# Summing the gathered value rows four units at a time, with seven row buffers and four weight buffers

## The chip, the core and the metric

The kernel runs on one core of a Trainium2 chip, as one launch. Its time is the device time of that core in microseconds (us). Five engines work in parallel and meet at semaphores: TensorE (PE in the profile; PEld is its weight load), VectorE (DVE), ScalarE (ACT), GpSimd (POOL) and SyncE (SP), which only issues loads. TensorE's granted clock can be 1.2 or 2.4 GHz; in this profile it is at the full 2.4 GHz through all of the stage that the change touches.

## What is computed

One step of a decoder layer, for 256 prompt tokens and for 8 x 4 sample tokens that read a paged cache of 2048 rows:

```python
h = rmsnorm(x); q, k, v, qi, ki, wi, cx, cb, cc, ga, gb = split(h @ w_in)
idx = top_k(relu(qi . ki) weighted by wi)            # 256 rows for each sample token
p   = softmax(q . k[idx] + bias)                     # 8 heads
out = sum over the 256 rows of p * v[idx]            # the step that is changed
x   = x + (sigmoid(ga) * (out @ w_pa) + sigmoid(gb) * (conv @ w_pb)) @ w_o
x   = x + square(relu(rmsnorm(x) @ w1)) @ w2
```

All of it is float32. The prompt's attention is dense with a mask, and is computed head by head.

## The kernel before

**The product with w_in.** h @ w_in is made in 44 pairs of column tiles (`pairs`, `win_half`, L397 and on), 256 columns each. A pair is eight chunks of the weights (128 x 512, two of the 16 rows of tiles). float32 is split into a high and a low part: ScalarE copies a chunk into its high part VH (`highs`, L849), and VectorE or GpSimd subtracts it to get the low part VL (`lows`, L1428 on VectorE, L1712 on GpSimd). TensorE then runs twelve matmuls of 288 columns on the chunk (L406 high x high, L407 high x low, L408 low x high). VH and VL have four buffers, so the high part of chunk u waits until chunk u - 4 is used. In pairs 30 to 37 VectorE makes the low parts of the odd chunks and GpSimd those of the even ones (`dve_low`). The SyncE queue loads the chunks of the next pair as the low parts of this one are done.

**The selected rows.** A sample token's 256 rows lie spread over the 128 partitions (4 partitions a token, 32 tokens) in 64 *units*: one unit is one row of 1024 floats in each partition, fetched by an indirect DMA of GpSimd (`gather`, L1715 and on, issued at L1726), 0.5 MB. First come 64 units of keys (up to pair 29), then 64 units of values. `kv` is a ring of five such row buffers (RK = 5). `knrep` and `vnrep` are two more tiles of that size, which hold the new keys and values of the sample tokens.

**Summing the values.** For unit v VectorE writes a *spread* (`spread_unit`, L1498): a tile `sp` of 128 x 256, in which the softmax weight of each partition stands in the column of its token and head. TensorE multiplies it with the rows (`unit_sum`, L780 to L785): eight heads, each a matmul with 32 columns of weights and 128 of data, accumulated in one bank; a head appears as two instructions in the trace (16 per unit, L783). `sp` is a ring of two. A unit zero, the new values in `vnrep`, comes ahead of unit 0.

**The order.** Everything is in the engines' program order. TensorE calls `after(j)` behind chunk j of each half of a pair, and `values_at` (L793) sums the units v - 1 and v behind every odd j: a group of two units behind every second chunk, 32 groups in pairs 30 to 37. After the second half of a pair (and at half of it) there are short attention matmuls of the prompt (L744, L745: logits; L391: transposes; L759, L760: output). VectorE goes through the same chunks c of a pair: behind every even c it writes two spreads, then the low parts up to chunk c + 3, then other work: in pair 30 the rest of a top-k over the mask (`prompt_top`), in pairs 31 and on at c = 1 and c = 5 the prompt's softmax (`prompt_row`, `prompt_scale`), in pairs 31 and 32 at c = 2, 3, 6 and 7 the convolution (`conv_tile`, L1533 to L1537) and at the end of 32 a product with the gate (L1565). The spread for unit v waits until unit v - 2 is summed. GpSimd makes the low parts up to chunk v + 4 of the stage and then issues the gather for unit v + 5 once unit v is summed. The semaphore `unit_summed` counts the sums, the one of `vnrep` included.

Of the kernel before, what the change touches and what calls it, by code (L numbers as in the profile page):

```python
# [13 lines left out]
P = 128  # L14
# [31 lines left out]
RK = 5  # L46
# [69 lines left out]
def build(nc, I, O):  # L116
    with ExitStack() as ctx:
# [54 lines left out]
        sp = sb("sp", [P, 2, H, NS])  # L172
# [86 lines left out]
        def const(name, rows=P):  # L259
# [19 lines left out]
            "unit_read conv_done tmax_ready tmax_turned tmax_wide tmax_back lg_shifted lg_exp lsum_ready lsum_wide "  # L279
# [5 lines left out]
        ks = [ctx.enter_context(nc.semaphore(f"rows_in{i}")) for i in range(RK)]  # L285
# [8 lines left out]
        C_MLP = C_WO + 16  # L294

# [89 lines left out]
        def _(pe):  # L385
# [377 lines left out]
            def tops(j):  # L763
                if j == 3:
                    pe.wait_ge(S["ul_copied"], 2)
                    pe.wait_ge(S["tmax_ready"], 1)
                    transpose(bank(4, 0, P, H), small[:, 0:H]).then_inc(S["tmax_turned"], 1)

            def sums(j):
                if j == 0:  # L770
                    pe.wait_ge(S["tmax_wide"], 1)
                    transpose(bank(7, 0, H), smx).then_inc(S["tmax_back"], 1)
                elif j == 3:
                    pe.wait_ge(S["lsum_ready"], 1)
                    pe.matmul(bank(5, 0, H), const("b4"), small[:, 16:16 + H], start=True, stop=True).then_inc(S["lsum_wide"], 1)
# [11 lines left out]
            def v_unit(v):  # L787
                n = UNITS + v
                pe.wait_ge(S["sp_ready"], v + 2)
                pe.wait_ge(ks[n % RK], 16 * (n // RK + 1))  # L790
                unit_sum((1 + v) % 2, kv[:, n % RK, :])

            def values_at(p, half):  # L793
                def after(j):
# [4 lines left out]
                    if j % 2 and v < UNITS:  # L799
                        v_unit(v - 1)  # L800
                        v_unit(v)
# [416 lines left out]
        def _(dve):  # L1218
# [264 lines left out]
            dve.tensor_reduce(small[:, 0:H], byh, AX_X, ALU.max).then_inc(S["tmax_ready"], 1)  # L1483
            lows(UNIT * (VP - 1) + 4)
            dve.wait_ge(S["tmax_turned"], 1)
            step(dve.tensor_reduce(smt, bank(4, 0, P, H).rearrange("p (n s) -> p n s", s=4), AX_X, ALU.max))
            dve.tensor_copy(smx.rearrange("p (n s) -> p n s", s=4), smt.unsqueeze(2).to_broadcast([H, NS, 4])).then_inc(S["tmax_wide"], 1)
            dve.wait_ge(S["tmax_back"], 1)
# [3 lines left out]
            dve.tensor_reduce(small[:, 16:16 + H], byh, AX_X, ALU.add).then_inc(S["lsum_ready"], 1)  # L1492
            dve.wait_ge(S["lsum_wide"], 1)
# [6 lines left out]
            def spread_unit(v):  # L1500

                if v:
                    dve.wait_ge(S["unit_summed"], v)
                spread((1 + v) % 2, lg[:, v, :].unsqueeze(2).to_broadcast([P, H, NS]))
# [359 lines left out]
```

## Time and profile before

| | |
|---|---|
| median of 3 runs | 1791.46 us (1788.7 to 1793.67) |
| profiled execution | 1791.65 us, span 1789.9 us |
| mean granted clock of TensorE | 0.990 |
| TensorE busy | 98% of the span |
| VectorE, ScalarE, GpSimd busy | 58%, 39%, 32% |
| moved by DMA | 348.53 MB, 195 GB/s over the span |
| value stage (first sum to the end of the last) | 509.3 to 664.0 us |

A row of the timeline gives the start in us from the start of the span, the duration, the engine, the line of the kernel, what is written and read, the shapes, and in brackets the idle time of the engine ahead of it with what ended it. Matmuls are pipelined: one starts while the one before it still runs, and the end of each is modelled, so the distance of the starts tells the pace, not the durations. "busy" of TensorE therefore also covers short breaks of its rhythm.

### The profile page before, as it was taken

The numbers are of one execution on the slowest core, as the hardware profiler recorded it, in microseconds if no ns is written. First come the engines' busy times: TensorE is split into PE (matmuls) and PEld (weight loads), VectorE is DVE, ScalarE is ACT, GpSimd is POOL, SyncE is SP. The second block draws the span as 40 slices with busy tenths as digits, with TensorE's granted clock in tenths as the row PEclk, the third lists the DMA queues.
The fourth block names the chain that finished last, engine by engine and source line by source line (L and its number), as shares of the span: only waits on it lengthen the run. The fifth ranks groups of instructions, "written<-read, shape, count | busy, mean of one in ns | idle before, by whom it ended". The sixth has DMA issues, their size and how long they took to land.

```text
span 1789.9 us, 32474 instructions
## 1 busy us (share of the span) xinstructions
PE 1751.0 (98%) x13712; PEld 1701.0 (95%) x13712; DVE 1039.0 (58%) x1147; ACT 690.1 (39%) x845; POOL 563.9 (32%) x450
## 2 busy tenths in 40 slices
PE   9999999999999999999999999999999999999997
PEld 8859998999888999999999999999999999999996
DVE  4559997889989432255456554455444554455543
ACT  5534443543344555433333332233323332233332
POOL 3718778888866667400231000000000000000001
PEclk9999999999999999999999999999999999999998
DMA  6725457988879974654454444444444444444442
GB/s 211 239 66 156 153 166 256 349 296 295 306 263 316 337 275 152 209 182 159 167 187 156 165 164 165 164 165 163 166 163 165 164 164 165 164 165 164 163 165 100
DMA packets 73793, 348.53 MB, mean 195 GB/s; under 512 B 8978, under 2 KB 11154, under 8 KB 52660
## 3 DMA queue, kind: packets, MB, share of 16 engines
q1 hardware_dynamic: 50112, 268.00, 44.0%
q0 software_dynamic: 19584, 71.31, 11.4%
q10 hardware_dynamic: 3988, 7.66, 1.2%
q8 instruction: 81, 1.33, 0.3%
q14 instruction: 28, 0.23, 0.0%
HBM read 340.50 MB, written 6.44 MB: 194 GB/s over the span
## 4 chain that ended last, share of the span: by engine, by line
PE 86%; DVE 10%; POOL 2%; DMA 1%; issue 1%; ACT 0%; POOLq 0%; DVEq 0%; ACTq 0%
PE PM L426 19%; PE PM L428 19%; PE PM L427 19%; PE PM L406 8%; PE PM L408 7%; PE PM L407 7%; PE PM L391 2%; DVE lg L1438 2%; DVE kv L1433 2%; DVE VL L1428 2%; PE PM L783 1%; DMA kv<-cache_v,offs 1%; POOL VL L1712 1%; POOL kv L1726 1%; DVE sp L1498 1%
## 5 line engine op out<-in xcount | busy, mean ns | idle before, releaser
L849 ACT ACTIVATE WH<-wring 128x2048 fp32r<-128x2048 f32 (+1 forms) x163 | 307.3, 1885 | 679.9 <-PE PM L428 676.1
L1582 DVE TENSOR_TENSOR WL<-wring,WH 128x2048 fp32r<-128x2048 f32 x159 | 364.5, 2292 | 341.3 <-ACT WH L849 341.2
L406 PE MATMUL PM<-hH,VH 128*128 128x288 f32 x1408 | 428.9, 305 | 11.1 <-POOL VL L1712 6.9
L1712 POOL TENSOR_TENSOR VL<-wring,VH 128x512 fp32r<-128x512 f32 x292 | 383.4, 1320 | 163.5 <-ACT VH L849 147.8
L407 PE MATMUL PM<-hL,VH 128*128 128x288 f32 x1408 | 418.7, 297 | 0.0
L408 PE MATMUL PM<-hH,VL 128*128 128x288 f32 x1408 | 417.3, 296 | 0.0
L426 PE MATMUL PM<-XH,WH 128*128 128x288 f32 x1280 | 379.1, 296 | 1.5 <-DVE WL L1589 1.5
L426 PE MATMUL PM<-YH,WH 128*128 128x288 f32 x1280 | 379.4, 296 | 0.0
L427 PE MATMUL PM<-YL,WH 128*128 128x288 f32 x1280 | 377.6, 295 | 0.0
L427 PE MATMUL PM<-XL,WH 128*128 128x288 f32 x1280 | 377.6, 295 | 0.0
L428 PE MATMUL PM<-XH,WL 128*128 128x288 f32 x1280 | 376.3, 294 | 0.0
L428 PE MATMUL PM<-YH,WL 128*128 128x288 f32 x1280 | 376.3, 294 | 0.0
L849 ACT ACTIVATE VH<-wring 128x512 fp32r<-128x512 f32 x352 | 221.7, 631 | 336.7 <-PE PM L408 336.2
L406 PEld LDWEIGHTS PM<-hH,VH 128*128 128x128 f32 x1408 | 267.2, 190 | 24.6 <-POOL VL L1712 8.9
L408 PEld LDWEIGHTS PM<-hH,VL 128*128 128x128 f32 x1408 | 268.2, 190 | 0.0
L407 PEld LDWEIGHTS PM<-hL,VH 128*128 128x128 f32 x1408 | 267.6, 190 | 0.2
L1767 POOL TENSOR_SCALAR ysam<-ysam,small 32x1024 f32<-32x1024 f32 x2 | 6.2, 3122 | 824.1 <-DVE small L1688 824.1
L426 PEld LDWEIGHTS PM<-XH,WH 128*128 128x128 f32 x1280 | 239.8, 187 | 1.8 <-ACT G L926 1.7
L428 PEld LDWEIGHTS PM<-XH,WL 128*128 128x128 f32 x1280 | 241.0, 188 | 0.0
L428 PEld LDWEIGHTS PM<-YH,WL 128*128 128x128 f32 x1280 | 241.0, 188 | 0.0
L427 PEld LDWEIGHTS PM<-XL,WH 128*128 128x128 f32 x1280 | 240.2, 188 | 0.1
L427 PEld LDWEIGHTS PM<-YL,WH 128*128 128x128 f32 x1280 | 240.2, 188 | 0.0
(267 smaller groups left out, 1574.4 us busy)
## 6 DMA issues: line engine op xcount, KB each, us to landing
wring<-w_in SPq DMA_DIRECT2D x176, 512.0 KB, 4.6
wring<-w_mlp_in SPq DMA_DIRECT2D x64, 1024.0 KB, 5.2
wring<-w_mlp_out SPq DMA_DIRECT2D x64, 1024.0 KB, 5.2
wring<-w_o SPq DMA_DIRECT2D x16, 1024.0 KB, 5.2
wring<-w_pb SPq DMA_DIRECT2D x8, 1024.0 KB, 4.9
wring<-w_pa SPq DMA_DIRECT2D x8, 1024.0 KB
xT<-x_t SPq DMA_DIRECT2D x1, 2304.0 KB, 12.2
bias_scratch<-uv ACTq DMA_DIRECT2D x8, 192.0 KB, 4.6
```

Source lines behind the costliest of these rows:

```text
L391: return pe.transpose(out, in_, cp[0:n, 0:n])
L406: pe.matmul(out, vh, hH[:, k, :], start=(k == 0), stop=False)
L407: pe.matmul(out, vh, hL[:, k, :], start=False, stop=False)
L408: m = pe.matmul(out, vl, hH[:, k, :], start=False, stop=(k == KT - 1))
L426: pe.matmul(out, wh, rh[:, k0 + k, :], start=(first and k == 0), stop=False)
L427: pe.matmul(out, wh, rl_[:, k0 + k, :], start=False, stop=False)
L428: m = pe.matmul(out, wl, rh[:, k0 + k, :], start=False, stop=(last and k == CK - 1))
L849: return act.activation(out, in_, ACT.Copy, **kw)
L1428: dve.tensor_tensor(VL[:, u % 4], r, VH[:, u % 4], ALU.subtract).then_inc(S["vl_dve"], 1)
L1433: m = dve.tensor_tensor(by2, by2, PM[:, 6:8, :], ALU.mult)
L1582: dve.tensor_tensor(WL[:, i % 2], wring[:, i % 2], WH[:, i % 2], ALU.subtract).then_inc(S["wl_ready"], 1)
L1712: pool.tensor_tensor(VL[:, u % 4], r, VH[:, u % 4], ALU.subtract).then_inc(S["vl_pool"], 1)
```

## The change

`sp` gets four buffers instead of two. TensorE sums four units behind chunk j = 3 of each half (16 groups) instead of two behind each odd chunk. VectorE writes four spreads at c = 0 and c = 4, each as soon as the unit four before it is summed. The value rows get seven buffers: the five of `kv`, then `knrep` and `vnrep` (`v_row`). GpSimd now issues the gather for unit v behind the low parts up to chunk v - 3 of the stage, once unit v - 7 is summed; units 5 and 6 are the first to go to `knrep` and `vnrep`. Seven semaphores of the softmax are replaced by two that count. No arithmetic is changed or moved to another engine.

```diff
@@ -169,7 +169,7 @@
-        sp = sb("sp", [P, 2, H, NS])
+        sp = sb("sp", [P, 4, H, NS])
@@ -276,13 +276,13 @@
-            "unit_read conv_done tmax_ready tmax_turned tmax_wide tmax_back lg_shifted lg_exp lsum_ready lsum_wide "
+            "unit_read conv_done soft_ready soft_turned lg_shifted lg_exp "
-        ks = [ctx.enter_context(nc.semaphore(f"rows_in{i}")) for i in range(RK)]
+        ks = [ctx.enter_context(nc.semaphore(f"rows_in{i}")) for i in range(RK + 2)]
@@ -292,6 +292,14 @@
+
+        def v_row(v):
+
+            r = v % (RK + 2)
+            if r < RK:
+                at = (UNITS + r) % RK
+                return kv[:, at, :], ks[at], 16 * (-(-(UNITS - at) // RK) + v // (RK + 2) + 1)
+            return (knrep if r == RK else vnrep)[:], ks[r], 16 * (v // (RK + 2) + 1)
@@ -763,16 +771,16 @@
-                    pe.wait_ge(S["tmax_ready"], 1)
-                    transpose(bank(4, 0, P, H), small[:, 0:H]).then_inc(S["tmax_turned"], 1)
+                    pe.wait_ge(S["soft_ready"], 1)
+                    transpose(bank(4, 0, P, H), small[:, 0:H]).then_inc(S["soft_turned"], 1)
...
@@ -785,10 +793,10 @@
                 m.then_inc(S["unit_summed"], 1)
             def v_unit(v):
-                n = UNITS + v
+                rows, arrived, count = v_row(v)
                 pe.wait_ge(S["sp_ready"], v + 2)
-                pe.wait_ge(ks[n % RK], 16 * (n // RK + 1))
-                unit_sum((1 + v) % 2, kv[:, n % RK, :])
+                pe.wait_ge(arrived, count)
+                unit_sum((1 + v) % 4, rows)
             def values_at(p, half):
                 def after(j):
@@ -796,9 +804,9 @@
                     if v == 0:
                         pe.wait_ge(S["sp_ready"], 1)
                         unit_sum(0, vnrep[:], True)
-                    if j % 2 and v < UNITS:
-                        v_unit(v - 1)
-                        v_unit(v)
+                    if j == 3 and v < UNITS:
+                        for i in range(4):
+                            v_unit(v - 3 + i)
                 return after
             for p in range(VP, AP0 + H + 1):
...
@@ -1499,9 +1507,9 @@
             def spread_unit(v):
-                if v:
-                    dve.wait_ge(S["unit_summed"], v)
-                spread((1 + v) % 2, lg[:, v, :].unsqueeze(2).to_broadcast([P, H, NS]))
+                if v >= 3:
+                    dve.wait_ge(S["unit_summed"], v - 2)
+                spread((1 + v) % 4, lg[:, v, :].unsqueeze(2).to_broadcast([P, H, NS]))
             def prompt_row(h):
@@ -1542,9 +1550,9 @@
             for p in range(VP, AP0 + H):
                 for c in range(UNIT):
                     v = UNIT * (p - VP) + c
-                    if c % 2 == 0 and v < UNITS:
-                        spread_unit(v)
-                        spread_unit(v + 1)
+                    if c % 4 == 0 and v < UNITS:
+                        for i in range(4):
+                            spread_unit(v + i)
                     lows(UNIT * p + c + 4)
                     if p == VP:
                         if c < TOPP // 8 - 2:
@@ -1714,17 +1722,24 @@
             def gather(n):
-                src, u = ("cache_k", n) if n < UNITS else ("cache_v", n - UNITS)
-                if RK <= n < UNITS + RK:
-                    k, added = n - RK, sum(m <= n - RK for m in ACT_UNITS)
+                if n >= RK:
+                    k = n - RK
+                    added = sum(m <= k for m in ACT_UNITS)
                     if k in ACT_UNITS:
                         pool.wait_ge(S["unit_added"], added)
                     else:
                         pool.wait_ge(S["unit_read"], k + 1 - added + (k > NEWKEY))
-                elif n >= UNITS + RK:
-                    pool.wait_ge(S["unit_summed"], u - RK + 2)
-                pool.indirect_dma_start(out=kv[:, n % RK, :], out_offset=None, in_=I[src],
-                                        in_offset=bass.IndirectOffsetOnAxis(ap=offs[:, u:u + 1], axis=0)).then_inc(ks[n % RK], 16)
+                if n < UNITS:
+                    pool.indirect_dma_start(out=kv[:, n % RK, :], out_offset=None, in_=I["cache_k"],
+                                            in_offset=bass.IndirectOffsetOnAxis(ap=offs[:, n:n + 1], axis=0)).then_inc(ks[n % RK], 16)
+                else:
+                    gather_v(n - UNITS)
+
+            def gather_v(v):
+
+                rows, arrived, _ = v_row(v)
+                pool.indirect_dma_start(out=rows, out_offset=None, in_=I["cache_v"],
+                                        in_offset=bass.IndirectOffsetOnAxis(ap=offs[:, v:v + 1], axis=0)).then_inc(arrived, 16)
             pool.wait_ge(S["scale_ready"], 1)
             for b in range(DB):
@@ -1739,9 +1754,13 @@
                 if n == 28:
                     pool.wait_ge(S["nat_done"], 12)
                     pool.memset(up[:, :, 0:2], 0.0).then_inc(S["pads_zero"], 1)
-            for v in range(0, UNITS - RK):
-                lows(UNIT * VP + v + 5)
-                gather(UNITS + RK + v)
+            for v in range(RK, UNITS):
+                if v == RK:
+                    pool.wait_ge(S["unit_read"], UNITS + 1 - len(ACT_UNITS))
+                else:
+                    lows(UNIT * VP + v - 2)
+                    pool.wait_ge(S["unit_summed"], v - RK)
+                gather_v(v)
             lows(C_MIX)
             def square_pairs(before, n0):
```

## Rows read from the trace of the kernel before

**Rows 1.** Page, part 1: busy us (share of the span) and instructions of each engine.

```profile
PE 1751.0 (98%) x13712; PEld 1701.0 (95%) x13712; DVE 1039.0 (58%) x1147; ACT 690.1 (39%) x845; POOL 563.9 (32%) x450
```

**Rows 2.** Busy us by stretch: PE, PEld, DVE, ACT, POOL; clock; DMA share; GB/s.

```profile
509.30:528.91 19.61, 16.81 (x229) 14.93 (x229) 18.23 (x50) 6.45 (x11) 11.15 (x11) 1.00 0.76 250
528.91:547.17 18.26, 18.26 (x232) 16.75 (x229) 16.95 (x42) 7.41 (x14) 13.35 (x13) 1.00 0.97 338
547.17:565.71 18.54, 18.54 (x235) 17.03 (x232) 18.08 (x42) 9.65 (x17) 13.51 (x13) 1.00 0.92 330
565.71:576.89 11.18, 10.18 (x124) 9.28 (x121) 10.62 (x24) 6.18 (x12) 5.46 (x6) 1.00 0.81 272
...
586.67:605.87 19.20, 19.20 (x239) 17.64 (x236) 8.10 (x20) 9.23 (x18) 12.84 (x12) 1.00 0.92 341
605.87:625.08 19.21, 19.21 (x239) 17.65 (x235) 8.51 (x21) 9.91 (x18) 12.15 (x12) 1.00 0.92 327
```

**Rows 3.** Timeline of TensorE around a group of two: start us, us, line, operands.

```profile
610.35 0.29 PE L408 MATMUL PM<-hH,VL 128*128 128x288 f32 x1
610.57 1.08 PE L783 MATMUL PM<-kv,sp 128*32 128x128 f32 x32
611.58 0.40 PE L406 MATMUL PM<-hH,VH 128*128 128x288 f32 x1
611.82 0.30 PE L407 MATMUL PM<-hL,VH 128*128 128x288 f32 x1
...
614.76 0.29 PE L408 MATMUL PM<-hH,VL 128*128 128x288 f32 x1
```

**Rows 4.** Timeline of TensorE, a group that a late row splits into single units.

```profile
638.88 0.64 PE L783 MATMUL PM<-kv,sp 128*32 128x128 f32 x16
639.83 0.65 PE L783 MATMUL PM<-kv,sp 128*32 128x128 f32 x16 [0.31 <-DMA kv<-cache_v,offs]
640.40 0.40 PE L406 MATMUL PM<-hH,VH 128*128 128x288 f32 x1
```

**Rows 5.** TensorE's waits in the stage: three rows of the timeline, one of its waits.

```profile
522.60 1.08 PE L783 MATMUL PM<-kv,sp 128*32 128x128 f32 x32 [0.83 <-DVE sp L1498]
...
571.49 1.08 PE L783 MATMUL PM<-kv,sp 128*32 128x128 f32 x32 [1.00 <-DVE sp L1498]
...
586.10 0.64 PE L783 MATMUL PM<-kv,sp 128*32 128x128 f32 x16 [0.48 <-DMA kv<-cache_v,offs]
...
PE PM L406 <- DVE VL L1428: 1.1, 1, 1.1
```

**Rows 6.** Timeline of VectorE in pairs 30 to 33.

```profile
510.03 0.43 DVE L1498 TENSOR_TENSOR sp<-cp,lg 128x256 f32<-128x256 f32 x1 [0.55 <-PE PM L783]
...
533.65 0.86 DVE L1498 TENSOR_TENSOR sp<-cp,lg 128x256 f32<-128x256 f32 x2 [0.78 <-PE PM L783]
...
536.66 1.31 DVE L1537 SCALAR_TENSOR_TENSOR zB<-uv,gcol,zB 128x32 f32<-128x32 f32 x1
...
571.68 0.68 DVE L1428 TENSOR_TENSOR VL<-wring,VH 128x512 fp32r<-128x512 f32 x1
```

**Rows 7.** Timeline of GpSimd: low parts (L1712) and gathers (L1726).

```profile
536.64 1.28 POOL L1712 TENSOR_TENSOR VL<-wring,VH 128x512 fp32r<-128x512 f32 x1 [0.46 <-ACT VH L849]
...
572.65 1.30 POOL L1712 TENSOR_TENSOR VL<-wring,VH 128x512 fp32r<-128x512 f32 x1 [4.82 <-ACT VH L849]
...
611.77 0.95 POOL L1726 DMA_INDIRECT kv<-cache_v,offs  x1 [0.62 <-PE PM L783]
613.02 0.93 POOL L1726 DMA_INDIRECT kv<-cache_v,offs  x1 [0.30 <-issue]
```

**Rows 8.** GpSimd's gathers in the stage: issue ns min/median/max, and their landing.

```profile
L1726 POOL DMA_INDIRECT kv<-cache_v,offs x59: 934/953/1395, 513.9 to 654.9; - x59
...
DMA to landing us min/median/max: 4.3/7.4/10.3
```

**Rows 9.** TensorE's waits from 665 to 1776 us: total us, times, longest.

```profile
PE PM L426 <- DVE WL L1589: 1.5, 1, 1.5
```

## What the change will do

> **What bounds the kernel now.** I read the page first. TensorE is busy for 98% of the span [rows 1], so only what shortens TensorE's own stream, or a wait in it, can move the time. The change touches one stage: the value units are summed between the weight chunks of pairs 30 to 37, from 509.3 to 664.0 us. The table by pair [rows 2] shows two regimes in it. In the first three pairs (509.30 to 565.71) VectorE is busy 18.23 of 19.61, 16.95 of 18.26 and 18.08 of 18.54 us: it is as full as TensorE. Later it needs only 8.5 of 19.2 us per pair and TensorE is alone on the path. After the stage TensorE streams on: from 665 to 1776 us it shows one wait, 1.5 us at the start of the mixing, and none of its rows names anything of this stage [rows 9]. So what the stage gains at its end stays gained.
>
> **What a group costs.** In [rows 3] the matmuls of the weight product start 2.94 us apart over 22 steps (611.82 to 614.76), 0.134 us each. At a group of two value units this rhythm is broken three times: last product matmul to first value matmul 0.22 instead of 0.134 (+0.09); value group to next product matmul 1.01; and then 0.24 to the one after it (+0.10). [Rows 4] have a group that a late transfer had split: its second half, one unit, takes 0.57 us from its start (639.83) to the next product matmul (640.40). So a unit costs 1.01 - 0.57 = 0.44 us, and a group has 0.57 - 0.44 = 0.13 us beside its units. A seam, in and out of the value matmuls, is 0.09 + 0.13 + 0.10 = 0.32 us whatever the number of units.
>
> **Part 1: four units per group.** 64 units make 16 groups instead of 32. The 16 groups that go are those at j = 1, with product matmuls on both sides, as in [rows 3]; those at j = 3 stay where they are, with the attention matmuls or the next half behind them. 16 x 0.32 = 5.1 us of TensorE's stream go; the matmuls themselves remain. Bounds: 0 (a longer group pays its seam again at each unit; rows 4 against rows 3 speak against it) and 5.3.
>
> **Part 2: waits in the stage.** Four waits of TensorE hang on VectorE: three times a group waits for its spread weights (idle 0.83 us at 522.60, the same at 527.90, 1.00 at 571.49; to each come 0.07, by which a matmul's modelled end, 0.29, overlaps the 0.22 of an undisturbed seam: 0.9, 0.9 and 1.1), and once, at 511 us, the product waits 1.1 us for a low part. Two hang on a gathered row: 639.83 - 638.88 - 0.44 = 0.5 us, and 0.7 at 586.10, whose idle time is 0.17 longer [rows 4, 5]. With four weight buffers VectorE writes the four of a group before the first of its four chunks, not before the last two, so none of the three waits on spreads can come back in that form. But VectorE's work is not less: the same 65 spreads of 0.43 us and the same low parts. In the first three pairs the path goes over to it. What then comes late is the low part of chunk 4g+3, which VectorE makes behind the four spreads at c = 4g. I follow it to the start of pair 33. In the trace the two spreads end at 571.68 [rows 6]. Before that VectorE idled for TensorE twice, 0.55 us at 510.03 and 0.78 us at 533.65 [rows 6]; both go, since unit 3's spread comes after two that need no wait, and at pair 31 the sums are done before VectorE gets there. Two spreads more have to be made by then (+0.8). That is 571.68 - 0.55 - 0.78 + 0.8 = 571.15; the low part behind them takes 0.68 [rows 6], so chunk 27 of the stage starts at about 571.8. It takes 12 x 0.134 + 0.09 = 1.7 us, the group behind it 0.57 + 3 x 0.44 = 1.89, and it ends at 575.4. The same point is at 576.89 now (boundary in rows 2). So of the 2.2 us of seams and the 2.9 us of waits on spreads in this stretch only 1.5 us come out at its end. At 511 us the first low part comes 0.4 us later (four spreads, not three, lie ahead of it); this is inside that VectorE account. Bounds of the 1.5 us: 0.3 if one more blocking by GpSimd (below) falls into it, 4.7 if VectorE keeps up.
>
> From there on VectorE has slack and the nine remaining groups of four (units 28 to 63) save 9 x 0.32 = 2.9 us.
>
> **Part 3: seven row buffers.** The two waits on rows were 1.2 us in all. The first came from a GpSimd gather held back: its low part waited 4.82 us for ScalarE, which itself waited for VectorE's last convolution product [rows 7]; the change asks of each gather the low parts of two chunks fewer (up to v - 3, not v - 1), so this one would not have been held. The tightest unit is now 4g+7: gathered when unit 4g is summed, read as the last of the next group. Gather issue follows the group's start by 611.77 - 610.57 = 1.2 us [rows 3, 7], landing takes 7.4 us (median of 4.3 to 10.3) [rows 8]: group start + 8.6. A pair will take 19.21 - 2 x 0.32 = 18.6 us, half of it 9.3 (8.8 and 9.8 in turn, by the attention matmuls between), and unit 4g+7 is 3 x 0.44 = 1.3 us into its group: needed at + 10.6, so 2.0 us to spare on the mean, 1.5 in the short half. Now an odd unit is needed 9.6 + 0.44 = 10.0 us after its release at the same 1.2 + 7.4, 1.4 to spare. I count the 1.2 us as saved; the bounds are 0 and 1.2. The mean rate rises from 327 to 327 x 19.21/18.6 = 338 GB/s, which the pair from 586.67 already had (341, at a DMA share of 0.92) [rows 2].
>
> The gathers move in GpSimd's order: it issues two, then makes the low part of chunk 4g+6, then two more. It starts the two at + 1.2 and + 2.45, each about 0.95 us [rows 7], the low part at + 3.5, done at + 4.8. TensorE wants that chunk after 1.89 us of group, 0.3 us of transposes and two chunks of 1.6 us: at + 5.5. Margin 0.7 us: nothing on the path, but thin; it costs if two gathers take the longest time seen (1.40 us, rows 8): 0.2 us a group, 3 us in all. The gathers for units 5 and 6 now go out before the first sums, into buffers that lie free; nobody waits for either, and they cost GpSimd two issues of 1.25 us beside its waits for ScalarE. One more gather between low parts at about 502 us meets a GpSimd that waits for ScalarE there anyway; I cost it at nothing, at most 0.3 us.
>
> The renamed semaphores keep the order of the softmax steps: nothing.
>
> **Sum.** 1.5 + 2.9 + 1.2 = 5.6 us off. The profiled execution took 1791.65 us (span 1789.9), 0.2 us above the median of 1791.46: 1791.65 - 5.6 = 1786.0, and 1785.9 from the median. I say 1786.0.
>
> **A port shared by VectorE and GpSimd.** VectorE's 32-column product L1537 takes 0.24 us at most places, but 1.31 when it starts at 536.66, 0.02 us behind a low part of GpSimd that lasts until 537.92 [rows 6, 7]. The Trainium skill, "SBUF — State Buffer" (SBUF: two separate sides), says why: a VectorE instruction with two SBUF inputs and a GpSimd one that reads SBUF lock each other out for the whole instruction. The trace agrees, 1.07 us a time. Spreads have two SBUF inputs as well, and there are now four in a row. By the rule each of the twelve GpSimd low parts of the three full pairs could cost VectorE 1.1 us; in VectorE's timeline eleven of them already do, so the rule adds one at most, the 1.2 us in my lower bound.
>
> **Rivals.**
> A. VectorE sets the pace of more than I think: in pairs 30 to 32 nothing is gained (0.3), the thin GpSimd margin costs half of its 3 us, and the row waits stay in part (0.6): 0.3 + 2.9 + 0.6 - 1.5 = 2.3 us off, 1789.3. For: VectorE's 97% in pair 32. Against: 1.3 us of its idle time goes for certain.
> B. VectorE keeps up: the seams count in full, and all waits but the one at 511 us go: 5.1 + 2.9 + 1.2 - 0.4 = 8.8 off, 1782.9. For: spreads are now due later. Against: its account above, since the low part of the fourth chunk stands behind them.
> C. The slower side: four gathers in a row queue up behind the weight loads, and unit 4g+7 lands late. If the landing rises from the 7.4 to the 10.3 us that is the longest now [rows 8], it is there at + 11.5, 0.9 late, in each of 15 groups: 13.5 us, net 7.9 slower, 1799.6. It outweighs the gain from a landing of 9.8 us on. For: DMA shares of 0.92 to 0.97 in [rows 2]. Against: the burst begins after a pause of about 3 us, so its first gather, the tight one, meets the emptiest queue.
> D. The seam isn't per group but per unit, so the change saves only waits: at most 2.7, 1789. Rows 4 speak against it.
>
> **Chances.** Forecast 0.55, A 0.20, B 0.12, C 0.07, D 0.06. Own range of the forecast: 1784 to 1788.5. The 80% range takes in B and A and leaves C out: 1782.5 to 1790.8. This kernel's runs lie between 1788.70 and 1793.67, so 0.3% (5.4 us, below 1786.1) is about what a measurement can tell from no change; my value lies on that line. Faster by more: all of B and not quite two thirds of the forecast, 0.46. Within: 0.46. Slower: C and a little noise, 0.08.
>
> **What would show it.** Sixteen groups of 64 value matmul records, about 1.7 us from first to last; a pair in the later half at 18.6 instead of 19.2 us; no wait of a value group on its spreads, but product matmuls of the fourth chunk waiting about 1 us on VectorE's low part in pairs 32 and 33; the stage's end, now 664.0, at about 658.5; nothing changed in length behind it. Wrong if value matmuls wait for rows in more than a few groups (C), if product matmuls wait for GpSimd's low part in most groups (A), or if VectorE idles in pairs 31 and 32 (B).

## Result: 0.3% slower, and the profile after

| | before | after |
|---|---|---|
| median of the runs, us | 1791.14 (1788.7 to 1795.26, 10 runs) | 1796.32 (1795.12 to 1799.35, 10 runs) |
| ratio after/before, 95% interval | | 1.003 [1.002, 1.004] |
| profiled execution, us (span) | 1791.65 (1789.9) | 1795.49 (1793.7) |
| first value matmul, us | 509.32 | 510.46 |
| start of the last value matmul, us | 663.82 | 667.62 |
| from there to the end of the span, us | 1126.1 | 1126.1 |

The 3.8 us between the two profiled executions all arise inside the stage or just ahead of it: 1.14 us at its start, 2.66 us in its length (154.50 to 157.16). The forecast was 5.6 us less, not 3.8 more.

In the changed kernel the product matmuls stand at L414 to L416, the value matmuls at L791, the spreads at L1506, the low parts at L1436 (VectorE) and L1720 (GpSimd), the value gathers at L1741. The page's first part, beside [rows 1]:

```profile
PE 1750.7 (98%) x13712; PEld 1704.0 (95%) x13712; DVE 1058.8 (59%) x1147; ACT 689.8 (38%) x845; POOL 562.4 (31%) x450
```

VectorE is busy 19.8 us longer with the same 1147 instructions: something makes them last longer. The table by stretch (columns and stretches as in [rows 2]):

```profile
510.46:528.09 17.63, 16.38 (x229) 15.14 (x228) 16.77 (x51) 6.43 (x11) 10.04 (x9) 1.00 0.72 252
528.09:550.99 22.90, 20.09 (x232) 18.23 (x228) 22.30 (x47) 8.91 (x15) 13.44 (x13) 0.93 0.88 313
550.99:571.61 20.62, 18.70 (x236) 17.29 (x232) 19.03 (x40) 8.79 (x16) 12.88 (x12) 1.00 0.87 290
571.61:583.17 11.56, 10.35 (x124) 9.44 (x120) 11.16 (x22) 4.94 (x12) 7.04 (x7) 1.00 0.81 256
...
592.51:611.37 18.86, 18.86 (x239) 17.79 (x235) 12.60 (x21) 9.80 (x18) 12.67 (x13) 1.00 0.95 333
611.37:629.92 18.55, 18.55 (x239) 17.71 (x236) 10.05 (x20) 9.81 (x18) 13.01 (x13) 1.00 0.96 340
```

Pair 30 got 1.98 us shorter than in [rows 2], pair 31 then 4.64 us longer and pair 32 2.08 us longer, with VectorE busy for 22.30 of 22.90 us; the two later pairs are 0.34 and 0.66 us shorter than theirs in [rows 2]. TensorE's waits in the stage (us in total, times, longest) and three of the four in its timeline:

```profile
PE PM L414 <- DVE VL L1436: 6.9, 4, 2.7
```

```profile
545.78 0.40 PE L414 MATMUL PM<-hH,VH 128*128 128x288 f32 x1 [2.68 <-DVE VL L1436]
...
567.93 0.40 PE L414 MATMUL PM<-hH,VH 128*128 128x288 f32 x1 [1.86 <-DVE VL L1436]
...
579.50 0.40 PE L414 MATMUL PM<-hH,VH 128*128 128x288 f32 x1 [1.21 <-DVE VL L1436]
```

No wait on spreads and none on a gathered row is left [rows 5]. The place is the forecast one, VectorE's low part of the fourth chunk, but the longest wait is in pair 31, where none was forecast, and the size is not the forecast one. A group of four, beside [rows 3]:

```profile
600.46 0.64 PE L791 MATMUL PM<-kv,sp 128*32 128x128 f32 x16
600.92 0.62 PE L791 MATMUL PM<-knrep,sp 128*32 128x128 f32 x16
601.36 0.62 PE L791 MATMUL PM<-vnrep,sp 128*32 128x128 f32 x16
601.80 0.62 PE L791 MATMUL PM<-kv,sp 128*32 128x128 f32 x16
```

The four units start 0.46, 0.44 and 0.44 us apart: no seam between them.

**Where VectorE's time goes.** GpSimd's timeline, and below it VectorE's, at two places of the changed kernel:

```profile
532.62 0.94 POOL L1741 DMA_INDIRECT kv<-cache_v,offs  x1 [0.31 <-issue]
533.58 1.29 POOL L1720 TENSOR_TENSOR VL<-wring,VH 128x512 fp32r<-128x512 f32 x1
...
540.10 0.95 POOL L1741 DMA_INDIRECT kv<-cache_v,offs  x1 [0.16 <-issue]
541.36 0.94 POOL L1741 DMA_INDIRECT kv<-cache_v,offs  x1 [0.30 <-issue]
542.32 1.28 POOL L1720 TENSOR_TENSOR VL<-wring,VH 128x512 fp32r<-128x512 f32 x1
...
532.99 2.32 DVE L1523 TENSOR_TENSOR scw<-scw,mask 128x384 f32<-128x384 f32 x1
...
540.61 0.48 DVE L1544 SCALAR_TENSOR_TENSOR zB<-uv,gcol,zB 128x256 f32<-128x256 f32 x1
...
541.74 1.92 DVE L1545 SCALAR_TENSOR_TENSOR zB<-uv,gcol,zB 128x32 f32<-128x32 f32 x1
```

L1545 lasts 0.24 us at most places. At 541.74 it starts 0.38 us into a gather and 0.58 us before the low part, and ends 0.06 us after the low part does: 1.92 us, 1.68 too long. L1523 at 532.99 is held in the same way, for 1.76 us. L1544 at 540.61 starts inside a gather as well, but one with another gather behind it, and takes its usual 0.48. In [rows 6] and [rows 7] the blocked product L1537 starts behind the start of the low part itself and lasts 1.31; ahead of that low part GpSimd waits 0.46 us for ScalarE. The changed order asks for each low part so late that its high part is mostly long there, and at the places shown GpSimd has no wait between gather and low part. GpSimd's waits for ScalarE's high parts in the whole stage (us in total, times, longest), first in the kernel before, then in the changed one:

```profile
POOL VL L1712 <- ACT VH L849: 32.4, 31, 4.8
```

```profile
POOL VL L1720 <- ACT VH L857: 8.0, 6, 3.3
```

Over the crowded stretch (pairs 30 to 32 and the first half of 33) I took each VectorE instruction's duration less that of the fastest of its line and shape. Where this is over 0.3 us I call it a *hit*. Before, 508 to 578 us: 12 hits, 11.8 us, none above 1.11. After, 508 to 582 us: 11 hits, 16.3 us, eight of them 1.68 to 1.77. Over the whole stage there are 15 hits, 13.9 us, before and 28, 33.6 us, after: this accounts for VectorE's 19.8 us more. The hits that are new in number lie behind the crowded stretch, where VectorE has slack.

The places shown are no single cases. From 495 to 672 us of the changed kernel 26 of VectorE's elementwise instructions (TENSOR_TENSOR and SCALAR_TENSOR_TENSOR) start inside a gather with a low part directly behind it. All 16 that start 0.29 us or more into the gather are hits, and none of the 10 that start in its first 0.25 us. Of the 46 that start inside a gather with another gather behind it none is a hit.

**The start of the stage.** First the changed kernel (GpSimd, then VectorE's copy in the softmax), then the same place before:

```profile
499.85 0.94 POOL L1741 DMA_INDIRECT knrep<-cache_v,offs  x1 [0.30 <-issue]
500.81 3.84 POOL L1720 TENSOR_TENSOR VL<-wring,VH 128x512 fp32r<-128x512 f32 x3
...
501.33 2.09 DVE L1495 COPY scw<-scw 8x128 f32<-8x128 f32 x1
```

```profile
499.43 2.52 POOL L1712 TENSOR_TENSOR VL<-wring,VH 128x512 fp32r<-128x512 f32 x2
...
501.21 0.82 DVE L1487 COPY scw<-scw 8x128 f32<-8x128 f32 x1
```

The gather of unit 5 delays three chained low parts; the copy then meets two of them, not the end of the second, and the transposes behind it, which stand in TensorE's order ahead of the next product matmuls, come 1.0 us later.

**The clock.** TensorE's stretches around the wait that ended at 545.78 (the clock is the third number from the end, a share of 2.4 GHz):

```profile
541.00:545.00 4.00, 2.10 (x16) 1.86 (x14) 3.93 (x8) 1.26 (x2) 2.27 (x3) 1.00 1.01 389
545.00:547.00 2.00, 1.22 (x7) 1.22 (x8) 1.96 (x7) 0.00 (x0) 0.00 (x0) 0.89 0.62 217
547.00:549.00 2.00, 2.00 (x19) 1.67 (x22) 1.89 (x7) 0.48 (x1) 0.00 (x0) 0.50 0.91 307
549.00:551.00 2.00, 2.00 (x58) 1.72 (x49) 1.89 (x7) 1.97 (x3) 0.96 (x2) 0.76 0.53 201
```

TensorE was without work for 2.68 us; about 1 us after it resumed the clock falls to 0.50 (1.2 GHz), and it is back within 4 us. Six product steps of 0.24 instead of 0.134 us and a group of 2.44 instead of 1.68 us make 0.64 + 0.76 = 1.4 us on top of the wait.

### The profile page after: what moved, and what is told of

The parts are those of the page before. It is cut to its first block, busy times and chain, and to the rows that moved or that the text cites. A ratio compares the mean times of both kernels' runs of the same rounds, so it can differ in the third digit from the quotient of the medians.

```text
span 1793.7 us, 32474 instructions
## 1 busy us (share of the span) xinstructions
PE 1750.7 (98%) x13712; PEld 1704.0 (95%) x13712; DVE 1058.8 (59%) x1147; ACT 689.8 (38%) x845; POOL 562.4 (31%) x450
## 4 chain that ended last, share of the span: by engine, by line
PE 86%; DVE 10%; POOL 1%; issue 1%; DMA 0%; ACT 0%; POOLq 0%; another core or an unknown queue 0%; DVEq 0%; ACTq 0%
PE PM L434 19%; PE PM L436 19%; PE PM L435 19%; PE PM L414 8%; PE PM L416 8%; PE PM L415 8%; PE PM L399 2%; DVE lg L1446 2%; DVE kv L1441 2%; DVE VL L1436 2%; PE PM L791 1%; DVE sp L1506 1%; POOL VL L1720 1%; POOL kv L1733 1%; DMA G<-x_prompt 0%
## 5 line engine op out<-in xcount | busy, mean ns | idle before, releaser
L414 PE MATMUL PM<-hH,VH 128*128 128x288 f32 x1408 | 427.7, 304 | 16.8 <-DVE VL L1436 8.4
L1720 POOL TENSOR_TENSOR VL<-wring,VH 128x512 fp32r<-128x512 f32 x292 | 382.5, 1317 | 140.6 <-ACT VH L857 124.0
L416 PE MATMUL PM<-hH,VL 128*128 128x288 f32 x1408 | 418.1, 297 | 0.1
L414 PEld LDWEIGHTS PM<-hH,VH 128*128 128x128 f32 x1408 | 267.4, 190 | 28.3 <-DVE VL L1436 9.9
L416 PEld LDWEIGHTS PM<-hH,VL 128*128 128x128 f32 x1408 | 268.5, 191 | 0.8 <-issue 0.6
```

What stands on the lines that cost most here:

```text
L414: pe.matmul(out, vh, hH[:, k, :], start=(k == 0), stop=False)
L416: m = pe.matmul(out, vl, hH[:, k, :], start=False, stop=(k == KT - 1))
L1720: pool.tensor_tensor(VL[:, u % 4], r, VH[:, u % 4], ALU.subtract).then_inc(S["vl_pool"], 1)
```

## Experiments

My theory after the result (Q in the expectations): a low part that is queued right behind a gather takes the port that VectorE and GpSimd share while the gather is still being issued, so a hit costs VectorE 1.7 instead of 1.1 us. The expectations call the first rival G: groups of four lose the time by themselves. The second is that the order of GpSimd's work loses it, whatever stands directly behind what. Each kernel is compared with the kernel before on its own chip. The stage is read from one profiled execution each, first to last value matmul, and the hits from the same one, from 508 to 582 us (so the kernel before shows one more than up to 578 us).

| run | median us (runs) | ratio, 95% | stage us | hits, us |
|---|---|---|---|---|
| before | 1791.14 (10) | 1 | 154.50 | 13, 12.2 |
| after | 1796.32 (10) | 1.003 [1.002, 1.004] | 157.16 | 11, 16.3 |
| e1_fence | 1784.64 (5) | 0.9955 [0.9942, 0.9969] | 147.74 | 11, 9.5 |
| e9_fence_again | 1788.67 (11) | 0.9986 [0.9977, 0.9994] | 150.97 | 12, 10.6 |
| e5_memset_no_wait | 1796.18 (12) | 1.0022 [1.0011, 1.0032] | 157.07 | 10, 16.0 |
| e2_before_queued | 1798.02 (8) | 1.0032 [1.0021, 1.0043] | 161.75 | 11, 18.4 |
| e6_before_fence | 1790.89 (12) | 0.9992 [0.9983, 1.0001] | 153.48 | 12, 10.9 |
| e3_order | 1792.04 (11) | 0.9996 [0.9987, 1.0005] | 152.99 | 13, 14.3 |
| e4_unit5_late | 1793.59 (11) | 1.0003 [0.9994, 1.0012] | 154.35 | 12, 17.5 |
| e12_fence_unit5 | 1794.99 (11) | 1.0016 [1.0007, 1.0025] | 158.05 | 10, 15.2 |
| e10_after_no_conv | 1786.66 (9) | 0.9967 [0.9955, 0.9979] | 148.41 | 12, 14.5 |
| e11_before_no_conv | 1790.32 (12) | 0.9995 [0.9986, 1.0003] | 152.74 | 7, 5.8 |
| e7_pairs_fence | 1788.72 (12) | 0.9975 [0.9967, 0.9984] | 151.73 | 10, 9.1 |
| e8_low_first | 1786.52 (10) | 0.9968 [0.9956, 0.9979] | 149.53 | 12, 11.6 |

### Something to wait for between gather and low part

The changed kernel, with a one-column memset on GpSimd behind a gather and a wait for it, ahead of the low part (`issued` is set by each value gather, `gather_v`). Nothing else moves. (Left out here are the lines that declare `fence`, `fences`, `issued` and the semaphore.)

```diff
                     if not dve_low(u):
+                        if issued[0]:
+                            issued[0] = False
+                            fences[0] += 1
+                            pool.memset(fence[:, 0:1], 0.0).then_inc(S["fenced"], 1)
+                            pool.wait_ge(S["fenced"], fences[0])
                         pool.wait_ge(S["vh_ready"], u + 1)
```

> The changed kernel, with one edit: in the value stage, between a gather and the low part that GpSimd has queued right behind it, stands a one-column memset, and GpSimd waits for it; so the low part is only handed to the engine when the gather's issue is over. Theory Q (a low part that is queued behind a gather keeps VectorE's two-input instructions out from early in the gather, 1.7 us each instead of 1.1): the blockings in pairs 30 to 33 fall back to at most 1.1 us, VectorE's chain to the start of pair 33 is about 5 us shorter, and the kernel takes 1789 to 1791.5. Rival G (it is the grouping by four itself: VectorE has to wait for a whole group before it can write the four spreads): blockings may shrink, but the stage ends as late as before the edit, 1795 to 1797. Rival P (the gather's own descriptor writing blocks VectorE): nothing changes, or it becomes worse by the memsets' time.

GpSimd, and the VectorE instruction beside it, in this kernel:

```profile
543.72 0.94 POOL L1750 DMA_INDIRECT vnrep<-cache_v,offs  x1 [0.30 <-PE PM L792]
544.66 0.11 POOL L1724 MEMSET fence<- 128x1 f32 x1
544.86 1.44 POOL L1728 TENSOR_TENSOR VL<-wring,VH 128x512 fp32r<-128x512 f32 x1
...
544.65 0.48 DVE L1545 SCALAR_TENSOR_TENSOR zB<-uv,gcol,zB 128x256 f32<-128x256 f32 x1
545.05 1.29 DVE L1546 SCALAR_TENSOR_TENSOR zB<-uv,gcol,zB 128x32 f32<-128x32 f32 x1
```

The low part starts 0.2 us later behind the gather, the hit is back at 1.05 us (1.29 instead of 0.24), no hit in the crowded stretch is above 1.11, and TensorE's waits on low parts shrink:

```profile
PE PM L415 <- DVE VL L1437: 3.2, 3, 1.5
```

The three are 1.2 us at the start and 0.47 and 1.54 us at the fourth chunk in pairs 32 and 33, near what the prediction had worked out for the change itself, about 1 us in each of these pairs. The stage takes 147.7 us; it forecast 154.5 - 5.6 = 148.9. The time came out below the expectation. The same kernel on another chip:

> The kernel with memset and wait once more, unchanged (1784.6 us before). In the traces of the changed kernel and of two experiments TensorE shows some 20 short pauses of 0.05 to 0.3 us among the first twelve product matmuls behind a group of four, 2 to 3 us in all; in this kernel's trace there are none. If they belong to the program, it shows none again and takes 1784 to 1786; if they come and go with the execution or the chip, it shows them in some runs and spreads up to 1788.

1788.67 us, stage 150.97. The gain over the kernel before holds (both intervals below 1), its size doesn't: 0.1% to 0.5%. The median is above the expectation, which allowed for 1788 us at most. By way of the kernel before it is 0.7% (first chip) and 0.4% (this one) faster than the changed kernel. The second trace has 21 short pauses of TensorE (below), as the changed kernel has, the first none, so the 0.4% is the comparison of like with like.

The memset alone, which waits only for the memset before it (the diff is against e1_fence):

```diff
                             issued[0] = False
+                            if fences[0]:
+                                pool.wait_ge(S["fenced"], fences[0])
                             fences[0] += 1
                             pool.memset(fence[:, 0:1], 0.0).then_inc(S["fenced"], 1)
-                            pool.wait_ge(S["fenced"], fences[0])
```

> As the kernel with the memset between gather and low part (1784.6 us), but GpSimd does not wait for this memset (only for the one before it, long done). The same instructions, in the same order; only the low part is again handed to the engine while the gather is being issued. Theory Q (what matters is that the low part is queued behind the gather): the blockings of 1.7 us are back and the time with them, 1794 to 1798. Rival M (the memset itself, or the later start of the low parts, is what helped): 1784 to 1787.

```profile
539.92 0.94 POOL L1751 DMA_INDIRECT kv<-cache_v,offs  x1 [0.31 <-issue]
540.86 0.11 POOL L1726 MEMSET fence<- 128x1 f32 x1
540.91 1.30 POOL L1729 TENSOR_TENSOR VL<-wring,VH 128x512 fp32r<-128x512 f32 x1
...
540.33 1.94 DVE L1546 SCALAR_TENSOR_TENSOR zB<-uv,gcol,zB 128x32 f32<-128x32 f32 x1
```

Nothing is healed: 1.70 us for this hit, the stage of the changed kernel, its time. So it is the wait that counts, not another instruction in between.

### The same in the kernel before

```diff
             for v in range(0, UNITS - RK):
-                lows(UNIT * VP + v + 5)
+                lows(UNIT * VP + v + 3)
                 gather(UNITS + RK + v)
```

Groups of two, five row buffers, two weight buffers; only GpSimd asks for its low parts two chunks later, so that their high parts are there.

> The kernel before (groups of two, two spreads, five row buffers), with one edit: GpSimd makes its low parts two chunks later in its own order, so that each low part stands right behind a gather, its high part long there. Theory Q: VectorE's blockings in pairs 30 to 32 grow from 1.1 to 1.7 us, eleven of them, and this alone makes the kernel 3 to 6 us slower than before (1794 to 1797). Rival G: no low part is needed earlier than it is made, so the time stays within 0.1% of before (1790 to 1793).

```profile
547.86 0.93 POOL L1726 DMA_INDIRECT kv<-cache_v,offs  x1 [0.30 <-issue]
548.80 1.31 POOL L1712 TENSOR_TENSOR VL<-wring,VH 128x512 fp32r<-128x512 f32 x1
...
548.15 2.26 DVE L1536 SCALAR_TENSOR_TENSOR zB<-uv,gcol,zB 128x256 f32<-128x256 f32 x1
```

Hits of 1.74 to 1.77 us, ten of eleven; the stage is 7.3 us longer than before, with 8.2 us of waits of TensorE on spreads in place of 2.7. The loss comes without any group of four. The time is 1 us above the expected 1794 to 1797; some of it is the slow clock again, 0.50 from 577 to 581 us, behind a wait of 3.03 us. The fence of e1_fence in the kernel before (a wait on the memset behind every value gather that a low part follows):

> The kernel before (groups of two, five row buffers) with the memset and its wait between a gather and the low part behind it. There most low parts already wait for their high part, so theory Q expects nothing to win in pairs 30 to 32: 1790.5 to 1792.5, stage 154 to 155 us long. If the memset helps by something else than the queueing, this kernel becomes as much faster as the changed one did (about 1780 to 1785).

There is little to heal, since its GpSimd waits for ScalarE there already: the stage is 1.0 us shorter, and the medians, 1.2 us apart, can't be told from equal.

### Other orders on GpSimd

```diff
-                    lows(UNIT * VP + v - 2)
+                    lows(UNIT * VP + v - (1, 2, 1, 0)[v % 4])
```

> The changed kernel with GpSimd's low parts in another place: low part of chunk 4g+6 ahead of the four gathers, that of 4g+8 behind the third. Both should then be waited for (their high part comes later than the gather ends), so that they aren't queued behind a gather. Theory Q: blockings of 1.1 us at most, as with the memset but without its cost: 1788 to 1791. Rival G: 1795 to 1797. It also tells whether rows then arrive late (the fourth gather leaves 1.3 us later).

In the changed kernel, one of GpSimd's two low parts per group comes two gathers earlier and the other one gather earlier, so that they meet a high part not yet there. It is half a cure, and slower than the expected 1788 to 1791 us: of 13 hits four still take 1.24 to 1.77 us, the start is still 1.0 us late, and one wait of 3.7 us is followed by a clock of 0.50. The next one moves only the first gather, behind the low parts up to the fourth chunk, and the last puts e1_fence's fence behind that one gather alone (the diff is against e1_fence):

```diff
                 if v == RK:
+                    lows(UNIT * VP + v - 1)
                     pool.wait_ge(S["unit_read"], UNITS + 1 - len(ACT_UNITS))
```

> The changed kernel with the gather of value unit 5 moved from ahead of the low parts at 500 us to just ahead of unit 6, as late as the free buffer allows without holding anything. In the changed kernel that gather pushes GpSimd's three low parts onto VectorE's copy in the softmax (2.09 us instead of 0.82), and the stage begins 1.15 us later. Theory: the copy falls back to about 0.8, the stage begins at 509.3 to 509.6 and the kernel is 0.7 to 1.3 us faster than the changed one: 1795.0 to 1795.6. Rival: the stage's start has another cause, no change (1796.3).

```diff
-                issued[0] = v >= RK
+                issued[0] = v == RK
```

> The changed kernel with the memset and its wait only once, behind the gather of value unit 5 at 500 us. In the changed kernel three low parts stand queued there and VectorE's copy in the softmax waits through two of them; with the wait the way from the last transposes ahead of the softmax to the first value sum should be 8.7 us as before and not 9.7: 0.8 to 1.3 us faster than the changed kernel, 1795.0 to 1795.5. Rival: this start is no part of the loss, 1796.3.

GpSimd and the copy in e12_fence_unit5:

```profile
503.34 0.94 POOL L1750 DMA_INDIRECT knrep<-cache_v,offs  x1 [0.30 <-issue]
504.28 0.11 POOL L1724 MEMSET fence<- 128x1 f32 x1
504.47 4.25 POOL L1728 TENSOR_TENSOR VL<-wring,VH 128x512 fp32r<-128x512 f32 x3
...
504.81 1.02 DVE L1496 COPY scw<-scw 8x128 f32<-8x128 f32 x1
```

From the first product matmul of the stretch (500.73 us in the changed kernel, 500.61 before) to the first value matmul it is 9.73 us in the changed kernel and 8.71 before. It is 8.7 us in all six kernels of seven row buffers in which a wait or another order parts this gather from the low parts (e1, e4, e7, e8, e9, e12), and 9.7 in the other three (e3, e5, e10). In both kernels the three low parts come as late behind the gather, and the copy starts inside the first of them. In the fenced one (0.34 us into it) it ends 0.1 us behind the first and takes 1.02 us; in the changed one (0.52 us into it) it ends 0.1 us behind the second and takes 2.09. So the first microsecond hangs on the same thing as the hits: whether GpSimd waits between the gather and the low parts. By itself it doesn't bring the time back: with the other fences missing the stage stays at 154.4 and 158.1 us. The median of e12 is as expected (1794.99 for 1795.0 to 1795.5), that of e4 is lower (1793.59 for 1795.0 to 1795.6); e4's trace lacks the short pauses that cost the changed kernel 2.5 us (below). The profiled execution of e12 is the slowest of its eleven runs, 1798.8 us. Most of that arises ahead of the stage: the product matmul that starts at 500.73 us in the changed kernel starts at 504.22 here. In the stage the clock is 0.50 from 548 to 554 us, longer than in the changed kernel, so the stage may read somewhat long too.

### VectorE out of the way

The convolution's tiles are left out on VectorE, in both kernels:

```diff
-                    elif p < VP + 3 and c in (2, 3, 6, 7):
-                        conv_tile(4 * (p - VP - 1) + 2 * (c // 4) + c % 4 - 2)
```

> The changed kernel with VectorE's convolution tiles left out (48 instructions in pairs 31 and 32; what reads their result gets other values). VectorE then has slack in pairs 31 and 32. Theory Q with VectorE on the path: the low parts queued behind gathers still block VectorE, but now this costs next to nothing, the stage is 148 to 151 us long (157.2 in the changed kernel), the kernel takes 1785 to 1789. Rival R (TensorE or the row transfers themselves suffer from the grouping by four): the stage stays above 154 us.

> The kernel before, with the same convolution tiles left out: the other half of the comparison. The prediction had a seam of 0.32 us per group, 5.1 us for the 16 groups, hidden in part by VectorE. With VectorE out of the way in both kernels, the stage should be 152.5 to 154 us long here, 4 to 5 us longer than in the changed kernel without the tiles, and 1 to 2 us shorter than in the kernel before with them (154.5).

TensorE's waits in the stage, first the changed kernel, then the one before, both without these tiles:

```profile
PE PM L414 <- DVE VL L1436: 1.2, 1, 1.2
```

```profile
PE PM L783 <- DVE sp L1498: 1.2, 2, 0.8
PE PM L406 <- DVE VL L1428: 1.2, 1, 1.2
PE PM L783 <- DMA kv<-cache_v,offs: 0.3, 1, 0.3
```

The hits are still there (14.5 us) and cost nothing, since VectorE has time. Now the change gains: the stage 4.3 us, the medians 3.7 us. That fits the seam: 5.1 us for 16 of them and 1.2 + 0.3 us of waits that end, less 1.9 us of short pauses, make 4.7.

### Groups of two or of four, once the fence is there

e7_pairs_fence is e1_fence with the groups, the order of the spreads and their two buffers as before (seven row buffers stay):

```diff
-                    if j == 3 and v < UNITS:
-                        for i in range(4):
-                            v_unit(v - 3 + i)
+                    if j % 2 and v < UNITS:
+                        v_unit(v - 1)
+                        v_unit(v)
```

> The changed kernel with memset and wait, seven row buffers and its order of gathers, but with groups of two again (two spreads ahead of every even chunk, two weight buffers in use). Against the same with groups of four (1784.6, stage 147.7 us) it prices the grouping alone. Seam theory: 16 seams of 0.32 us come back, 5.1 us, of which VectorE's pace hides some 2 in pairs 30 to 33, and the waits on late spreads return: 1788 to 1791. Rival D (the seam is not per group): 1784 to 1786.

e8_low_first is e1_fence with VectorE's late low part ahead of the four spreads (the diff is against e1_fence):

```diff
                     if c % 4 == 0 and v < UNITS:
                         for i in range(4):
+                            if v:
+                                lows(UNIT * p + c + 4)
                             spread_unit(v + i)
```

> The kernel with groups of four, memset and wait (1784.6 us), and at every fourth chunk VectorE makes the low part of chunk 4g+3 ahead of the four spreads instead of behind them. My account says that this low part is what TensorE still waits for in pairs 32 and 33 (3.2 us in all in that kernel's trace) and that the spreads, due only behind that chunk, have room: 1.35 us earlier each time, so 1.5 to 3 us faster, 1781.5 to 1783.3. Rival: VectorE's whole load is the bound in those pairs, and the spreads then come late instead: 1784 to 1786.

Groups of two with a fence take 1788.72 us, stage 151.73. The kernel before with a fence (e6_before_fence) took 1790.89 us on the same chip, so the seven rows and GpSimd's order are worth 2.2 us, 0.12%. Groups of four with a fence, on two other chips, have stages of 147.7 and 151.0 us and the ratios 0.9955 and 0.9986, one on either side of the 0.9975 of the groups of two. So what the grouping by itself is worth once the fence is there is not settled; the one comparison on the same chip, e8 against e7, gives 2.2 us in its favour, with the low part moved as well.

With the low part first only the 1.2 us at the start are left of the waits on VectorE, as meant, yet the time is no better (1786.52, expected 1781.5 to 1783.3): 22 short pauses take 3.2 us. They look like this, in the changed kernel behind a group of four:

```profile
640.63 0.19 PEld L414 LDWEIGHTS PM<-hH,VH 128*128 128x128 f32 x1
640.96 0.19 PEld L415 LDWEIGHTS PM<-hL,VH 128*128 128x128 f32 x1
...
640.76 0.29 PE L414 MATMUL PM<-hH,VH 128*128 128x288 f32 x1
640.96 0.40 PE L415 MATMUL PM<-hL,VH 128*128 128x288 f32 x1
641.20 0.30 PE L416 MATMUL PM<-hH,VL 128*128 128x288 f32 x1
```

The weight load at 640.96 starts 0.33 us behind the one before it, though its data is there and nothing is waited for; the steps beside it are 0.20 and 0.24 instead of 0.134. They stand within the first dozen product matmuls behind a group. Counting steps more than 0.05 us over 0.134, the changed kernel has 21 (2.5 us, without those of the slow clock), e8 22 (3.2), e9 21 (3.0), e10 16 (1.9); e5 and e12 have them too. No kernel with groups of two has one. Nor have e1, e3 and e4, which sum four at a time, apart from single steps behind waits and the slow clock. These three ran on one chip (with e2), e5 to e12 on two others: the pauses seem to go with the chip, and e1 against e9 is the same program with and without them. What they are stays open.

## Why the prediction was wrong

- **The seam: right.** 64 value matmuls in 1.68 us, 0.20 to the next instruction, the later pairs shown take 18.86 and 18.55 us, forecast 18.6. With VectorE out of the way the stage is 4.3 us shorter.
- **Part 3, rows: right.** No value matmul waits for a row. Rival C, late rows, did not come; nor D, a seam per unit.
- **Part 2, the step that failed** is VectorE's account, at "the rule adds one at most, the 1.2 us in my lower bound". I had counted how often GpSimd's low parts block VectorE and taken the price of each, 1.1 us, as fixed. In the crowded stretch the count hardly changed (12 to 11). The price rose to 1.7 us, because the diff took away the wait for ScalarE between gather and low part; with a wait put back there it is at most 1.11 again (e1_fence), and without one it is 1.74 to 1.77 in ten of eleven hits in the kernel before too (e2_before_queued). I had noted that each gather asks for two chunks fewer, and used this only in its favour. To the start of pair 33 the account reads: forecast end of the four spreads 571.15 (the two before end at 571.68), measured 578.76, 7.6 us late. Of these 6.0 are hits (15.9 instead of 9.9 us in this stretch), 1.14 the late start, 1.16 a new wait of VectorE for a group at 552.64 us, itself late by waits and clock; the rest is -0.7.
- **"One more gather between low parts at about 502 us … at most 0.3 us": wrong**, it was 1.0 us. I had read GpSimd's own waits there, not what its low parts hold up on VectorE: the softmax copy.
- **What the waits cost: missed.** About 1 us of wait at a time was forecast, and the sum has no term for the clock; behind 2.68 us of wait the slow clock cost 1.4 us more.
- **The sum.** The forecast was 5.6 us less, the two profiled executions show 3.8 us more: 9.4 us apart. The group of units 24 to 27 ends at 583.17, forecast 575.4: 7.8. Behind that the stage gained 2.5 of the forecast 2.9 + 1.2 us. Of the missing 1.6 us eight short pauses are 0.8; the rest I can't assign.
- **Rivals.** A came nearest in kind, VectorE sets the pace; it lay 3.3 us above the forecast, the result 9.4. The kernel did get slower, but none of my rivals had it slower for this reason.

The Trainium skill, "SBUF — State Buffer" (SBUF: two separate sides), says that the port pair which VectorE and GpSimd share is an exclusive lock, which goes to whoever starts first, for the whole instruction. Here the low part's record starts 0.58 us after VectorE's instruction that it blocks: by the record VectorE came first and should have gone through. "Perfetto Trace Analysis" (DMA Instruction — SWDGE) of the Trainium skill has the descriptors of a GpSimd DMA written by two of GpSimd's processors. The notes of its section GPSIMD Engine Instruction say that GpSimd's processors aren't synchronized beyond what an instruction does itself. By that the processors that write no descriptors would already start the low part queued behind the gather. The runs fit this (a wait between the two heals it, a memset without one doesn't, a gather behind a gather blocks nobody), but none of them shows which processor does what: it is argued, not shown.

## What to carry to other kernels

Counting how often two engines collide isn't enough. Look at what stands directly ahead of the blocking instruction in its own queue, and what a removed wait had been doing there. On GpSimd, where VectorE works near its limit, try a wait that really ends after the gather (here a one-column memset and its semaphore, 0.2 us) between an indirect DMA and a two-input operation. And before moving work to a fuller engine's account, ask what it costs if each term of it is half as much again: here a gain of 1.5 us stood on twelve hits.

## What was not expected of the hardware

- A GpSimd subtraction queued directly behind an indirect gather blocks VectorE's two-input instructions from about 0.6 us before its own record starts: 1.7 us a hit, 1.05 with a fence. The softmax's one-input fp32 copy of 8 x 128 is held as well (2.09 us against 0.82 and 1.02).
- After TensorE had idled 2.68 us its clock was at 0.50 for some 3 us, 1.4 us of loss; after waits of 0.83 and 1.00 us in the kernel before [rows 5] the stretches show 1.00 [rows 2], and after the 1.86 us at 567.93 as well. The length of the wait alone doesn't settle it: in e4_unit5_late a wait of 3.21 us that ended at 542.61 left the clock at 1.00, one of 2.50 us that ended at 564.76 was followed by 0.50.
- Short pauses of TensorE behind 64 small matmuls in 1.7 us, none behind 32: up to 3.2 us in a stage of 150, present for a program on one chip and absent for it on another. Cause open.
- The fastest version measured is the changed kernel with the fence: 1784.64 us on one chip; on a second it took 1788.67, against 1792.03 and 1791.59 for the kernel before on the same ones.
